# The second norm of a transformer-like block, done by halves of the tokens

## What is computed

```python
x = x + g1 * mix                       # mix = merged @ w_out
x = x + g2 * _swiglu(_modulate(_rms_norm(x, norm2_g[l]), sh2, sc2), w_ffn_in[l], w_ffn_out[l])

def _rms_norm(x, g):
    xf = x.astype(jnp.float32)
    y = xf * lax.rsqrt(jnp.mean(xf * xf, axis=-1, keepdims=True) + NORM_EPS)
    return (y * g.astype(jnp.float32)).astype(x.dtype)
def _modulate(h, shift, scale):
    return h * (1 + scale) + shift
def _swiglu(u, w_ffn_in, w_ffn_out):
    gate, up = jnp.split(u @ w_ffn_in, 2, axis=-1)
    return (jax.nn.silu(gate) * up) @ w_ffn_out
```

## Time and profile before

| what | us |
|---|---|
| median of 3 runs | 2595.86 |
| the three runs | 2593.07, 2595.86, 2596.41 |
| the profiled execution's own time | 2595.01 |
| its span, first to last instruction | 2593.0 |
| TensorE busy | 2558.2 (99%) |
| VectorE busy | 1974.1 (76%) |
| ScalarE busy | 1218.0 (47%) |
| mean granted clock of TensorE | 0.996 |

### The profile page before, as it was taken

The page is one execution under the profiler, slowest core; times in us unless marked ns, Lnnn a source line. Parts: engine busy times, 40 slices in busy tenths (PEclk is TensorE's granted clock), DMA queues, the critical chain, the costliest instruction groups (busy, mean ns, idle before and its releaser), DMA issues.

```text
span 2593.0 us, 38180 instructions
## 1 busy us (share of the span) xinstructions
PE 2558.2 (99%) x14069; PEld 2186.8 (84%) x14069; DVE 1974.1 (76%) x2182; ACT 1218.0 (47%) x1411; POOL 205.6 (8%) x277
## 2 busy tenths in 40 slices
PE   6999999999999999999999999999999999999998
PEld 4688888878888888888888888888888888888887
DVE  4467888778999999777867777878777767787443
ACT  4224887355555555322444444444444445455433
POOL 0011000100001111111000000000000000011000
PEclk9999999999999999999999999999999999999999
DMA  9976333855556666999568888888878864656543
GB/s 367 382 262 213 110 113 120 310 204 157 160 162 162 162 162 146 326 333 332 156 159 203 204 200 201 206 201 203 204 194 207 204 240 139 163 133 189 199 163 146
DMA packets 527975, 524.73 MB, mean 202 GB/s; under 512 B 16456, under 2 KB 466832, under 8 KB 523152
## 3 DMA queue, kind: packets, MB, share of 16 engines
q1 hardware_dynamic: 479152, 379.70, 47.2%
q0 software_dynamic: 44176, 126.90, 20.8%
q10 hardware_dynamic: 4560, 16.95, 1.7%
HBM read 427.00 MB, written 54.53 MB: 186 GB/s over the span
## 4 chain that ended last, share of the span: by engine, by line
PE 89%; DVE 4%; DMA 4%; issue 1%; ACT 1%; ACTq 0%; SPq 0%; DVEq 0%; POOL 0%; POOLq 0%
PE main L1754 17%; PE aux L1754 17%; PE main L1761 9%; PE aux L1761 9%; PE main L1437 7%; PE main L1438 6%; PE main L1439 6%; PE aux L1979 3%; PE aux L1978 3%; PE aux L1977 3%; DMA ada_pa<-in_w_ada 2%; DVE ada_acc L2114 1%; PE main L1979 1%; PE main L1978 1%; PE main L1977 1%
## 5 line engine op out<-in xcount | busy, mean ns | idle before, releaser
L2456 DVE TENSOR_TENSOR l_S<-f_S,h_S 128x1024 fp32r<-128x1024 f32 x288 | 344.5, 1217 | 15.2 <-ACT h_S L1055 15.2
L2456 DVE TENSOR_TENSOR l_A<-f_A,h_A 128x1024 fp32r<-128x1024 f32 x216 | 263.1, 1220 | 100.8 <-ACT h_A L1055 86.4
L1055 ACT ACTIVATE h_A<-f_A 128x1024 fp32r<-128x1024 f32 x216 | 226.7, 1052 | 219.8 <-PE aux L1761 111.6
L1055 ACT ACTIVATE h_S<-f_S 128x1024 fp32r<-128x1024 f32 x288 | 288.9, 1052 | 74.1 <-DVE f_S L2444 48.6
L1754 PE MATMUL main<-t_both,h_S 128*128 128x512 f32 x864 | 207.9, 389 | 0.2 <-DVE u_hi_spare L2509 0.2
L1754 PE MATMUL aux<-t_both,h_S 128*128 128x512 f32 x864 | 207.8, 389 | 0.0
L825 ACT ACTIVATE w_hi<-w_raw 128x1024 fp32r<-128x1024 f32 x120 | 125.4, 1053 | 170.7 <-DMA w_raw<-in_w_out 59.6
L1437 PE MATMUL main<-u_both,w_hi 128*128 128x512 f32 x508 | 201.4, 396 | 0.1
L2104 DVE TENSOR_TENSOR w_lo<-w_raw,w_hi 128x1024 fp32r<-128x1024 f32 x120 | 145.9, 1220 | 72.9 <-ACT w_hi L825 72.8
L1438 PE MATMUL main<-u_both,w_hi 128*128 128x512 f32 x508 | 198.5, 391 | 0.0
L1439 PE MATMUL main<-u_both,w_lo 128*128 128x512 f32 x508 | 197.9, 390 | 0.0
(11 more groups left out here) (363 smaller groups left out, 5593.3 us busy)
## 6 DMA issues: line engine op xcount, KB each, us to landing
f_A<-in_w_ffn_in SPq DMA_DIRECT2D x120, 512.0 KB, 5.0
f_S<-in_w_ffn_in SPq DMA_DIRECT2D x80, 512.0 KB, 6.0
f_S<-f_A POOLq DMA_DIRECT2D x80, 512.0 KB, 6.0
f_A<-in_w_in SPq DMA_DIRECT2D x72, 512.0 KB, 4.9
ada_pw<-in_w_ada POOLq DMA_DIRECT2D x64, 512.0 KB, 6.0
bw_f<-in_w_ffn_out SPq DMA_DIRECT2D x56, 512.0 KB, 7.0
w_raw<-in_w_in SPq DMA_DIRECT2D x48, 512.0 KB, 4.5
ada_pc<-in_w_ada SPq DMA_DIRECT2D x48, 512.0 KB, 7.6
```

What stands on the lines that cost most here:

```text
L1055: act.activation(wh[v][:, :, :], wf[b][v][:, :, :], ACT.Copy).then_inc(w_hi_done, 1)
L2456: dve.tensor_tensor(wl[b][v][:, :, :], wf[b][v][:, :, :], wh[v][:, :, :].bitcast(F32), ALU.subtract).then_inc(w_lo_done, 1)
```

## The change

Tokens are dealt with in two halves, the late half (`TOKENS[0]`, tokens 256 to 511) first.

- The last pair of the output projection (`out_halves`): each matmul is made as two of 256 columns, late half into `main`, early half into `aux` banks 0 and 2. Units 0 and 1 do both halves in turn; then units 2 and 3 do the late half of both banks, then the early half.
- Squares are folded: `sq_acc`'s two rows become one, VectorE adds the squares of tiles 14 and 15 to it by halves, and TensorE sums it with two one-column matmuls a half (`square_sums`). Root, reciprocal, diagonals and spread (`spread`) are done by halves as well. The filler is gone.
- The sums of the late half stand in TensorE's queue inside the early half of the last pair; those of the early half inside the first tiles of the feed-forward network. The first four tiles are scaled, split and multiplied half by half.
- Three chunks (13, 14, 15) move into VectorE's work on tiles 4, 5 and 6, chunk 12 behind the residual of row 14's late half. The last part of the gate goes by `part_sums(7)`, `sums_evac(8)` and `turn_sums(5)`, `mod2_out` on VectorE comes later.
- The splits of units 2 and 3 are done ahead of (ScalarE) or just after (VectorE) the scaling of tile 4, those of units 4 and 5 ahead of tile 10 on ScalarE, after the low part of tile 9 on VectorE.

```diff
 # ScalarE
-            for k in range(KT):
-                act.wait_ge(v_aff, k + 1)
+            act.wait_ge(sq_first, 1)
+            row_square(14, 0)
+            act.wait_ge(pair_free[1], Q_OUT // 2 + 4)
+            row_square(15, 0)
+            hi(G_OUT, 8, 3, 9)
+            half_root(0)
+            half_high(0, 0)
+            act.wait_ge(sq_first, 2)
+            row_square(14, 1)
+            half_high(1, 0)
+            act.wait_ge(sq_first, 3)
+            row_square(15, 1)
+            half_high(2, 0)
+            half_high(3, 0)
+            half_root(1)
...
+            for k in range(UC):
+                half_high(k, 1)
+            for k in range(UC, KT):
+                if k in (4, 10):
+                    for u in range(2):
+                        hi(G_FF0, 16, 0, 2 + u + 2 * (k // 10))
+                act.wait_ge(v_aff, UC + k + 1)
                 act.activation(u_hi[:, k, :], v_f[:, k, :], ACT.Identity, bias=mod2[:, 16 + k:17 + k]).then_inc(v_hi, 1)
-                if k in (1, 9):
-                    for u in range(2):
-                        hi(G_FF0, 16, 0, 2 + u + k // 4)
+                if k == 9:
+                    sums_evac(8, 2, sums_row2)
 # TensorE
+            def square_sums(s):
+                pe.wait_ge(sq_added, 9 + 2 * s)
+                if s:
+                    pe.wait_ge(rms_ready, 1)
+                for t in range(2 - 2 * s, 4 - 2 * s):
+                    ins = pe.matmul(aux[:, 3, t:t + 1], sq_acc[:, 0, t * P:t * P + P], ones[:, 0:1], start=True, stop=True)
+                ins.then_inc(ms_ready, 1)
+            def spread(s):
+                pe.wait_ge(mid_diag, s + 1)
+                roots = diag2[:, 2 - 2 * s:4 - 2 * s, :].rearrange("p t n -> p (t n)")
+                pe.matmul(aux[:, 1 - s, 0:TH], ones[:, :], roots, start=True, stop=True).then_inc(mid_spread, 1)
+            def out_halves():
...
+                for k in range(2):
+                    pe.wait_ge(lo_done, splits(G_OUT, 8, 3, 4 + k))
+                    for n in range(2):
+                        for cc in range(UC):
+                            for s in range(2):
+                                ins = half_triples(k, n, s, cc)
+                    ins.then_inc(unit_used, 1)
+                for s in range(2):
+                    for n in range(2):
+                        for k in range(2, 4):
+                            if s == 0 and n == 0:
+                                pe.wait_ge(lo_done, splits(G_OUT, 8, 3, 4 + k))
+                            for cc in range(UC):
+                                ins = half_triples(k, n, s, cc)
+                            if s and n:
+                                ins.then_inc(unit_used, 1)
+                            if s and not n and k == 2:
+                                square_sums(0)
+                        if not (s and n):
+                            ins.then_inc(half_done, 1)
+                        if s and not n:
+                            spread(0)
 # TensorE, up_first
-                for k in range(3):
+                pe.wait_ge(lo_done, splits(G_FF0, 16, 0, 1))
+                for s in range(2):
+                    for c in range(UC):
+                        pe.wait_ge(v_lo, UC * s + c + 1)
+                        for p in range(2):
+                            for n in range(2):
+                                ins = triple(main[:, 2 * p + n, TOKENS[s]], p, c, n, u_hi[:, c, TOKENS[s]], u_lo[:, c, TOKENS[s]],
+                                             s == 0 and c == 0, False, True)
+                            if s and c == UC - 1:
+                                ins.then_inc(unit_used, 1)
+                            if s == 0 and p == 0 and c == 1:
+                                square_sums(1)
+                            if s == 0 and p == 0 and c == 2:
+                                spread(1)
+                for k in range(1, 3):
                     pe.wait_ge(lo_done, splits(G_FF0, 16, 0, 2 * k + 1))
...
+                    if k == 1:
+                        part_sums(7, 0, True, 2)
+                turn_sums(5, sums_row2, aux[:, 2, :])
 # VectorE
+            dve.wait_ge(sq_added, 6)
+            dve.tensor_tensor(sq_acc[:, 0, :], sq_acc[:, 0, :], sq_acc[:, 1, :], ALU.add).then_inc(sq_added, 1)
+            dve.wait_ge(rows_landed[4], 96)
+            dve.wait_ge(half_done, 1)
+            half_residual(14, 0).then_inc(sq_first, 1)
+            next_chunk(3, 12)
+            lo(G_OUT, 8, 3, 8)
+            dve.wait_ge(half_done, 2)
+            half_residual(15, 0).then_inc(pair_free[1], 1)
+            add_squares(14, 0)
+            add_squares(15, 0)
+            half_diag(0)
+            lo(G_OUT, 8, 3, 9)
             dve.wait_ge(mid_spread, 1)
+            half_scale(0, 0)
+            dve.wait_ge(half_done, 3)
+            half_residual(14, 1).then_inc(sq_first, 1)
+            half_scale(1, 0)
+            half_low(0, 0)
+            add_squares(14, 1)
+            half_scale(2, 0)
+            half_low(1, 0)
+            dve.wait_ge(unit_used, G_OUT + 32)
+            half_residual(15, 1).then_inc(sq_first, 1)
+            half_low(2, 0)
+            half_scale(3, 0)
+            add_squares(15, 1)
+            half_low(3, 0)
+            half_diag(1)
+            dve.wait_ge(mid_spread, 2)
+            half_scale(0, 1)
+            for k in range(UC):
+                if k + 1 < UC:
+                    half_scale(k + 1, 1)
+                half_low(k, 1)
+            v_scale(UC)
+            for u in range(2):
+                lo(G_FF0, 16, 0, 2 + u)
+            for k in range(UC, KT):
                 if k + 1 < KT:
                     v_scale(k + 1)
...
+                if 4 <= k < 7:
+                    next_chunk(3, 9 + k)
+                if k == 9:
                     for u in range(2):
-                        lo(G_FF0, 16, 0, 2 + u + k // 4)
+                        lo(G_FF0, 16, 0, 4 + u)
```

More of the change, by code:

```diff
@@ L72 @@
 ORDER = ("A11", "S2", "S1", "A22", "A12", "S3", "S4")
+TOKENS = (slice(TH, T), slice(0, TH))
+NV = KT + UC
 NG = (NPAIR - KT) // 4
@@ L1201, in out_steps @@
             def out_steps(i, first=False, last=False):
-                for u in range(8):
+                for u in range(7 if last else 8):
                     if not first or u >= 2:
@@ L1206, in out_steps @@
                         sums_evac(7, 3, sums_row2)
-                    if u == 3 or (u == 7 and not last):
+                    if u in (3, 7):
                         j = u // 4
@@ L1439, in triple, with unit @@
                 return pe.matmul(dst, wl, m_hi_ap, start=False, stop=stop, skip_group_check=shared)
-            def unit(base, per, i, u, p, moving, first, last):
+            def unit(base, per, i, u, p, moving, first, last, shared=False):
                 pe.wait_ge(lo_done, splits(base, per, i, u))
@@ L1447, in unit @@
                         ins = triple(main[:, 2 * p + n, :], u % RING, cc, n, h, l,
-                                     first and cc == 0, last and cc == UC - 1)
+                                     first and cc == 0, last and cc == UC - 1, shared)
                 ins.then_inc(unit_used, 1)
@@ L1845, in out_first @@
                 ins.then_inc(unit_used, 1)
[L1847 to L1858, removed]
@@ L1928, in up_first @@
+                for k in range(1, 3):
                     pe.wait_ge(lo_done, splits(G_FF0, 16, 0, 2 * k + 1))
                     for c in range(UC):
[L1930 to L1936, removed]
-                                        pe.matmul(main[:, 2 * p + n, :], (w_hi, w_lo, w_hi)[piece][:, p, 0, n * P:n * P + P],
-                                                  (u_hi, u_hi, u_lo)[piece][:, 0, :], start=(piece == 0), stop=False)
-                            continue
@@ L2611, in residual, with next_chunk @@
                                                 mod2[:, ds(k, 1)], x_res[:, j, n, :], ALU.mult, ALU.add)
+            def next_chunk(i, cc):
+                dve.wait_ge(ada2_landed[cc % 4], i * 64 + (17 + cc // 4) * 16)
+                if cc == 0:
+                    dve.wait_ge(acc_used, i + 4)
+                chunk(ada2_pw[:, cc % 4, :], i * 16 + (64 + cc) if cc else 0, cvec[:, cc, 0:1])
             def out_steps(i, first=False, last=False):
-                for u in range(8):
-                    if (not first or u >= 2) and not (last and u == 7):
+                for u in range(6 if last else 8):
+                    if not first or u >= 2:
                         lo(G_OUT, 8, i, u + 2)
@@ new lines, in half_low, with v_scale @@
+            def half_low(k, s):
+                cols = TOKENS[s]
+                dve.wait_ge(v_hi, UC * s + k + 1)
+                dve.scalar_tensor_tensor(u_lo[:, k, cols], v_f[:, k, cols], mod2[:, 16 + k:17 + k],
+                                         u_hi[:, k, cols].bitcast(F32), ALU.add, ALU.subtract).then_inc(v_lo, 1)
+            def v_scale(k):
```

(3 more changed lines are left out.)

128 lines of the change are left out of this document (56 added, 72 removed).

## The result

The changed kernel takes 2599.86 us (median of 14 runs, 2597.47 to 2605.90) against 2596.27 for the kernel before (14 runs, 2593.07 to 2605.76). The ratio is 1.0016, with an interval of [1.0009, 1.0023]: 4.2 us slower, between 2.3 and 6.0. The forecast was 2599.0. The profiled execution took 2597.47 us, its span is 2595.4, against 2595.01 and 2593.0.

The account below looks back on a forecast made before the run. TensorE, busy 99% of the span, bounds the kernel. Costs of 4.9 plus waits make 11.4 us against 9.78 won; rounded to +1.7 with the turn, plus 1.5 for the clock, 2595.86 + 3.2 = 2599.0 us, range 2593.2 to 2602.5.

Parts of the forecast that it names:

- case A: TensorE waits before the third feed-forward quarter and its clock falls: 1.7 + 1.5 = +3.2 us, chance 0.55.
- Halves: Last bank and first four feed-forward tiles: 256-column matmuls take 0.1198 us each; 144 pairs cost +1.87 us.
- First wait: At the late half's square sums, TensorE waits 1.4 us for VectorE and ScalarE.
- Second wait: At the early half's square sums, inside the first feed-forward tiles, TensorE waits 0.7 us.
- First product: The first feed-forward product starts at 1238.80 instead of 1244.59, 5.8 us earlier.
- Tile 4: At the first full low part, after two splits on VectorE, TensorE waits 0.3 us.
- The long wait: Before the third quarter, ScalarE's gate-sum copy holds up two splits: 4.70 us from sum to product, 4.05 idle.
- Start of the third quarter: The third feed-forward quarter (k=2) starts at 1268.05 against 1266.59, +1.46 us.
- The clock: Behind or within the idle time before the third quarter, clock at 0.50 for 3.4 us, losing 1.5 (1.2 to 1.7).
- rival D: Clock also falls at the first sums, perhaps staying low twice as long after the long wait: +4.9 to +6.6, chance 0.13.
- Rival B: The wait before the third quarter comes but the clock does not fall: +1.7 us, 2597.6, chance 0.20.
- rival C: No long wait before the third quarter, ScalarE reaches the splits in time: -2.4 us, 2593.5, chance 0.12.

Follow-up runs that it names:

- split_ahead: The changed kernel with ScalarE's copy of the eighth sum moved behind the splits of units 4 and 5, just ahead of tile 11's high part: 2593.05 us, ratio 0.9989.
- warm_wait: The changed kernel with seven 256-wide filler matmuls into an unused bank behind the eighth sum: 2596.18 us, ratio 1.0001.
- sum_early: The changed kernel with TensorE issuing the eighth sum one tile earlier, ahead of tile 7: 2595.84 us, ratio 0.9993.
- as_changed: The changed kernel timed again with no edit: 2598.44 us, ratio 1.0009 against the kernel before.
- best: The changed kernel with the gate-sum copy after tile 11, units 4 and 5 split around tiles 7 and 8, output-weight low split behind squares: 2593.01 us, ratio 0.9986.
- packed_gate: The kernel before with only its eight gate columns and their filler replaced by the packed sum and the turn: 2597.45 us, ratio 1.0004.

## Why the prediction was right

The time, the mechanism and its place came as forecast (case A). That the time came so near is in part luck: the waits were priced too high and the clock too low, and the two errors worked against each other. Step by step, for the profiled changed kernel:

- **Halves.** Forecast 0.1198 each; measured 17.27 / 144 = 0.1199 (1212.99 to 1230.26). The prediction set this against the formula of the Trainium skill (TensorE: Matmul & The Clock Gate, "Back-to-back issue gap") and said that the trace does not agree. That was a misreading: the section gives the formula for isolated matmuls and says that in a stream with a load of weights before each the spacing differs, and this is such a stream. The sum doesn't use it.
- **First wait.** Forecast 1.4, measured 0.54: the wait most wrong. (The profile counts idle time from the modelled end of the last matmul, 0.16 behind the step that I counted with; by steps it is 0.7 against 1.4.) I had let chunk 11 wait 0.51 for its DMA "as now" on VectorE. In this trace the chunks run one behind the other and the chain arrives earlier:

```profile
1225.04 2.67 DVE L2154 SCALAR_TENSOR_TENSOR ada_acc<-ada_pw,cvec,ada_acc 128x1024 f32<-128x1024 f32 x2
...
1230.95 0.47 DVE L2686 SCALAR_TENSOR_TENSOR mixed<-main,mod,x_res 128x256 f32<-128x256 f32 x1
...
1231.91 0.42 DVE L2693 TENSOR_TENSOR sq_acc<-sq_acc,sq 128x256 f32<-128x256 f32 x1 [0.15 <-ACT sq L1227]
```

  The residual of row 15 starts at 1230.95, 17.96 us after the last bank's first matmul; I had 1231.94 and 1213.30, 18.64 us. In the other traces with this order the wait is 0.71, 0.87, 1.13 and 1.35: it moves with how far TensorE happens to be ahead of VectorE's backlog. The DMA is not the whole of it: in split_ahead chunk 11 did wait for it, 0.43, and TensorE 0.87; in warm_wait it did not wait, and TensorE waited 1.35. 1.4 was its upper end, not its middle.
- **Second wait** 0.7, measured 0.52. **First product** 5.8 us earlier, measured 6.6; the difference is the first wait's. **Tile 4** 0.3, measured 0.39. The unseen prices, a plain add (0.33 for 256 columns, 0.60 for 512) and a scale over two banks (0.66), came out as taken: an iteration with a chunk is 2.52 (1251.16 to 1253.68).
- **The long wait.** Forecast 4.70 from the sum to the next product with 4.05 idle; measured 4.48 and 3.84. Of the 0.2, 0.05 lies at the start of the copy (0.71 after the sum's, forecast 0.76) and 0.11 between the copy and the first split (0.28; forecast 0.39, from the earlier trace rows). That the order of the queue is the reason is shown by split_ahead and sum_early.
- **Start of the third quarter.** Forecast +1.46, measured +0.67 (53.96 against 53.29): the first wait again. From the first product on it was 29.25 by the forecast and 29.27 in the trace; there the small errors cancel.
- **The clock.** Forecast one fall, 1.5; measured one fall and 1.76 here, a fall with a low stretch twice as long and 2.8 in as_changed. Both lie above the bounds of 1.2 to 1.7: in this trace none of the low stretch lay in the idle time. The second half of the long stretch was the latter half of rival D, to which I gave it only together with an early fall. It can come by itself: one trace of two has it, and how often it comes isn't known.

The sum: +0.67 + 1.76 + 0.27 = +2.7, against the +3.2 of the forecast; too much wait, a little too little clock. Rival B (no fall) and rival C (no wait) are out in both traces of the change. warm_wait has the wait without the fall (stretch +1.92, where B had +1.7), and split_ahead nearly no wait (-1.77, where C had -2.4).

The stretch of +2.7 to +3.9 lies between the two timings of the changed kernel, 4.2 us [2.3, 6.0] and 2.3 us [0.0, 4.9], and in both intervals; nothing asks for a further cause, though a small one can't be excluded. What stays open: Why the clock stays low once or twice as long behind the same wait is not known. The price of the halves is read from the traces; no kernel that changes them alone was run. Of the two waits at the sums the best kernel attacks the first and still has 0.47 there; the second, 0.52, was not attacked.

## What to carry to other kernels

Before moving a step, read each in-order queue that it passes: an instruction that waits for the bottleneck engine's own next result must not stand ahead of work that the same engine needs first. When such a wait is left on TensorE, price it as its idle time plus the slow clock behind it (here 3.8 plus 1.8 to 2.8 us), and try the cheap cure first, the order of two instructions on another engine. Splitting a phase by halves to hide a serial chain brought the next phase's start 6.6 us forward (0.6 of it from the gate columns, if the packed_gate run carries over) at 1.9 us of dearer matmuls in all. As first written it lost 2 to 4 us; only when the helpers' queues stood in the order of the new schedule was the kernel faster, by 3.6 us [1.3, 6.0] at best.

## What the runs showed of the hardware that was not expected

The filler of the kernel before is worth 3.6 us, though without it TensorE's waits are only 0.79 and 1.48 us long: the clock stood at 0.50 for 10.1 us, three times the 3.4 us of other places, with TensorE "busy" for 8.62 of them, in part with one-column sums. It fell at 1242.6, at the end of the second row sums, before the longer wait had begun; ahead of it stood sixteen one-column records and the 0.79 us. The length of one wait alone does not say whether the clock falls. In packed_gate, where the row sums have their filler, 1.69 us idle in one piece left it at 1.00; one trace each, so this is an observation and not a rule. The single waits of 0.4 to 1.35 us among the dense halves cost it nothing in any of the six traces that have them (the changed kernel twice, split_ahead, sum_early, warm_wait, best): it is 1.00 from 1225 to 1262 in all. And after the same idle 3.84 us the clock was low for 3.42 us in one execution and 6.83 in another: 1 us of difference between two executions of the same instructions.
